# Second layer's square-ReLU inputs: two weight slots as one group, by an exact scheme of 26 block products

## The reference

```python
def sq_relu_mlp(h, w1, w2):
    return jnp.square(jax.nn.relu(h @ w1)) @ w2
# in layer l = 1
h = rmsnorm(x, norm2_g[l]) * (1.0 + sc2) + sh2
x = x + g2 * sq_relu_mlp(h, w_mlp1[l], w_mlp2[l])     # w1: 1024 x 4096, w2: 4096 x 1024
```

## Time and profile before

| | |
|---|---|
| median of 3 runs | 3288.65 us (3288.53 to 3288.9) |
| the profiled execution's own time | 3284.69 us |
| its span, first to last instruction | 3282.9 us |
| granted TensorE clock, mean | 0.999 |
| TensorE busy | 3250.7 us (99%), 15522 instructions |
| VectorE busy | 1972.2 us (60%) |
| GpSimd busy | 1031.4 us (31%) |
| ScalarE busy | 729.2 us (22%) |
| mean DMA rate | 93 GB/s |

### The profile page before, as it was taken

One profiled execution on the slowest core, in us unless ns is written; L12 is line 12 of the kernel. 1 busy time (PEld: TensorE's weight loads), 2 busy tenths in 40 slices (PEclk: granted clock), 3 DMA queues, 4 the chain that ended last, 5 costly groups with the idle time before them and its releaser, 6 DMA issues. The chain is left out here.

```text
span 3282.9 us, 40266 instructions
## 1 busy us (share of the span) xinstructions
PE 3250.7 (99%) x15522; PEld 2459.8 (75%) x15522; DVE 1972.2 (60%) x3598; ACT 729.2 (22%) x1567; POOL 1031.4 (31%) x806
## 2 busy tenths in 40 slices
PE   8999999999999999999999999999999999999999
PEld 5767775555555566788888854888886887888888
DVE  8766677676765624288545656655436588855443
ACT  3432422010101333131111124211101235321111
POOL 0111323323232010224444401444441553344443
PEclk9999999999999999999999999999999999999999
DMA  7334412333331121332222221222222221122222
GB/s 270 131 100 131 123 52 82 111 123 111 119 106 55 61 89 49 98 86 80 88 90 90 88 80 64 87 81 90 90 90 103 82 83 49 40 77 90 90 90 90
DMA packets 66895, 304.50 MB, mean 93 GB/s; under 512 B 8496, under 2 KB 21168, under 8 KB 40720
## 3 DMA queue, kind: packets, MB, share of 16 engines
q1 hardware_dynamic: 54368, 268.68, 24.1%
q0 software_dynamic: 6528, 18.75, 1.8%
q10 hardware_dynamic: 5808, 14.49, 1.3%
HBM read 292.84 MB, written 2.88 MB: 90 GB/s over the span
## 5 line engine op out<-in xcount | busy, mean ns | idle before, releaser
L2855 POOL TENSOR_TENSOR scratch<-ring 128x512 f32<-128x512 f32 (+1 forms) x160 | 226.7, 1417 | 1437.9 <-PE psum L744 957.4
L744 PE MATMUL psum<-big,scratch 128*128 128x256 f32 (+1 forms) x2240 | 606.9, 427 | 0.0
L744 PEld LDWEIGHTS psum<-big,scratch 128*128 128x128 f32 x2240 | 425.8, 190 | 163.5
L744 PE MATMUL psum<-H,scratch 128*128 128x256 f32 (+1 forms) x2144 | 498.9, 387 | 0.0
L744 PEld LDWEIGHTS psum<-H,scratch 128*128 128x128 f32 x2144 | 406.7, 190 | 76.9 <-issue 5.0
L744 PE MATMUL psum<-big,ring 128*128 128x256 f32 (+1 forms) x1584 | 421.5, 419 | 6.6 <-DVE cb L2172 2.5
L744 PE MATMUL psum<-H,ring 128*128 128x256 f32 (+1 forms) x1536 | 396.3, 400 | 1.7 <-issue 0.7
L744 PEld LDWEIGHTS psum<-big,ring 128*128 128x128 f32 x1584 | 300.3, 190 | 111.8 <-DVE cb L2172 3.7
L1480 ACT ACTIVATE cb<-psum 128x256 f32<-128x256 f32 x336 | 128.8, 383 | 1010.9 <-PE psum L744 1010.9
L744 PEld LDWEIGHTS psum<-H,ring 128*128 128x128 f32 x1536 | 290.2, 190 | 76.6 <-ACT H L1578 6.4
L713 PE MATMUL psum<-H,ring 128*128 128x512 f32 x736 | 329.6, 598 | 0.0
(11 more groups left out here) (395 smaller groups left out, 4168.5 us busy)
## 6 DMA issues: line engine op xcount, KB each, us to landing
ring<-in_wall SPq DMA_DIRECT2D x202, 1024.0 KB, 4.8
big<-in_wada SPq DMA_DIRECT2D x48, 512.0 KB, 3.5
big<-in_wada POOLq DMA_DIRECT2D x32, 512.0 KB, 4.2
big<-in_wada SPq DMA_DIRECT2D x8, 1024.0 KB, 21.1
scratch<-in_rpb ACTq DMA_DIRECT2D x16, 512.0 KB, 4.1
big<-big ACTq DMA_DIRECT2D x64, 64.0 KB, 5.1
X<-in_xin SPq DMA_DIRECT2D x4, 768.0 KB, 6.7
scratch<-negd SPq DMA_DIRECT2D x8, 384.0 KB, 9.5
```

The lines of the kernel that those rows point to most:

```text
L744: mm = pe.matmul(fast_bank(st, q, b), lhsT, rhs(k), start=start and k == 0, stop=k == kt - 1, skip_group_check=True)
L2855: pool.tensor_tensor(s1, a21, a22, ALU.add).then_inc(combo_own, 1)
```

## The change

Of the second layer's MLP the 16 "in" slots are taken as eight groups of two (`GROUPED`, `grouped_stage`); the 16 "out" slots stay as they are, and so does the first layer's MLP (`MLP[0]`).

A group is a product of a 4 x 4 grid of weight blocks (256 rows by 128 columns; rows in four parts, the 512 columns of two slots in four) with a 4 x 2 grid of input blocks (256 features by 256 tokens). It is done with 26 products of two matmuls each, and three kinds of sums:

- **inputs** (`mix_blocks`, VectorE): 18 mixed inputs of 512 columns, made inside `norm`, one after scaling 4, one after 5, one after 6, the rest after the last. They replace the 16 of 256 columns.
- **weights** (`group_weights`, GpSimd): per group 18 operations, four of 512 columns and 14 of 256, each waiting by `used(n)` until the group before has done product n with the buffer, and by `formed(n)` for its own earlier results. The ring slots of a group hold seven and six blocks of 256 columns instead of eight (1.7 MB for two). SyncE loads a further 1.3 MB of blocks (`group_terms`) and GpSimd's queue adds 0.79 MB onto them with an accumulating transfer (`accum_op`). Third form and later need its result. The ring slots are released after form 7 and form 16.
- **results**: 13 copies by ScalarE and 20 sums by VectorE per group, then eight squares and eight differences by VectorE (ScalarE's relu goes away). Products and their results use all eight banks.

TensorE's order and waits stand in `group_begins` and `group`; `group_begins` of the next group comes directly behind the group, or, behind a round's "out" slots, ahead of the last slot's last product. GpSimd's order in a round is: forms of the even group, forms of the odd group, then the four "out" slots' combinations. The rotary helper buffers move from "big" to "wx", `mixed_ready` and the counters of fast slots are renumbered, and some semaphores are shared with earlier uses.

The diff, cut to what sets the order ("..." marks what is left out):

The banks of the result chains, and TensorE's opening of a group and its product:

```diff
+chain_banks = dict(k=1, g=0, o=0, q=0, d=2, b=5, e=3, f=6, c=7, a=4)
...
+    def group_begins(st, g):
+        pe.wait_ge(group_form, W_FORMS0 + W_FORMS * g + 3)
+        if g:
...
+        times(w13, h_block(3, 1), "k")
+        if g:
+            pe.wait_ge(group_added, ADDS0 + ADDS * (g - 1) + 14)
+        times(pair_sums(g)[3], h_block(3, 0), "g")
...
+    def times(weights, inputs, to, start=True):
+        for k in range(2):
+            mm = pe.matmul(chain(to), weights[:, k * P:(k + 1) * P], inputs[:, k, :], start=start and k == 0, stop=k == 1,
+                           skip_group_check=True)
+        mm.then_inc(group_product, 1)
```

TensorE's group from product 3 on (cut):

```diff
+def group(st, g):
...
+    if g:
+        pe.wait_ge(group_added, added + 8)
+    else:
+        pe.wait_ge(h_ready, st.h0 + 4)
+    times(one21, h_block(2, 1), "d")
+    mixed(1)
+    if g:
+        pe.wait_ge(group_added, added + 13)
+    times(s03, hK, "b")
+    mixed(3)
+    if g:
+        pe.wait_ge(group_added, added + 20)
+    if after_fast:
+        pe.wait_ge(c11_done, after_fast)
+    times(w3, h3, "e")
...
+    pe.wait_ge(group_form, forms + 5)
+    pe.wait_ge(group_copied, copies + 2)
+    times(w0, hA, "g", False)
...
+    times(w14, hE, "a")
+    mixed(6)
+    pe.wait_ge(group_form, forms + 8)
+    pe.wait_ge(group_added, added + ADDS + 1)
+    times(w21, hD, "o")
...
+    mixed(16)
+    pe.wait_ge(group_added, added + ADDS + 4)
+    times(one02, h9, "q")
...
+    pe.wait_ge(group_form, forms + 18)
+    times(w7, h_block(3, 1), "e", False)
```

TensorE's order over a round:

```diff
+def grouped_stage(st):
+    group_begins(st, 0)
+    for c in range(4):
+        group(st, 2 * c)
+        group_begins(st, 2 * c + 1)
+        group(st, 2 * c + 1)
+        w.slot += 4
+        w.grouped += 4
+        fast_stage(st, None, lambda x, i: group_begins(st, 2 * c + 2) if x == 8 * c + 7 < 31 and i == 7 else None,
+                   range(8 * c + 4, 8 * c + 8))
```

What the first "out" slot of a round waits for, in TensorE's `fast_stage`:

```diff
+if st.grouped():
+    signal = {5: hid_first}.get(i, signal)
+    return lambda k, kt: pe.wait_ge(signal, st.pairs(g)) if k == 0 else None
```

VectorE's group (cut; `ready` waits for a product, a copy or a sum, `own.wait` for its own last results):

```diff
+def relu2(x, added):
+    ready(added=added)
+    own(dve.scalar_tensor_tensor(x, x, 0.0, x, ALU.max, ALU.mult))
...
+ready(product=6, copied=5)
+minus(part_m, copy_e, chain("g"))
...
+ready(product=19)
+minus(part_m, part_m, chain("d"))
+ready(product=20)
+minus(lo1[1], lo1[1], chain("f"))
+ready(added=8)
+plus(lo1[0], part_m, lo1[0])
+ready(added=9)
+minus(lo1[1], lo1[1], part_o)
+ready(copied=13)
+plus(hi1[1], copy_l, hi1[1])
+ready(product=21)
+plus(part_q, chain("b"), copy_i)
+ready(product=22, added=13)
+minus(part_m, chain("q"), part_q)
+plus(part_o, part_o, part_q)
+ready(added=14)
+plus(hi0[0], part_m, hi0[0])
+ready(added=15)
+minus(hi0[1], part_o, hi0[1])
+relu2(lo0[0], 6)
+relu2(lo0[1], 7)
+own.wait()
+dve.tensor_tensor(t0[0], lo0[1], lo0[0], ALU.subtract).then_inc(hid_first, 1)
+ready(product=24)
+plus(hi1[0], chain("c"), hi1[0])
+relu2(lo1[0], 10)
+relu2(lo1[1], 11)
+own.wait()
+dve.tensor_tensor(t1[0], lo1[1], lo1[0], ALU.subtract).then_inc(hid_first, 1)
+ready(added=18)
+plus(hi1[0], hi1[0], copy_j)
+relu2(hi0[0], 16)
+relu2(hi0[1], 17)
+own.wait()
+own(dve.tensor_tensor(t0[2], hi0[1], lo0[1], ALU.subtract))
+dve.wait_ge(hid_first, pair + 1)
+own.wait()
+dve.tensor_tensor(t0[1], hi0[1], t0[0], ALU.subtract).then_inc(hid_mid, 1)
+ready(product=26)
+minus(hi1[1], chain("e"), hi1[1])
+dve.sem_inc(hid_last, 1)
+dve.wait_ge(hid_mid, pair + 1)
+dve.tensor_tensor(t0[3], hi0[0], t0[1], ALU.subtract).then_inc(hid_mixed, 1)
```

VectorE's mixed inputs (cut), called by `norm` after each scaling:

```diff
+def mix_blocks(st, part):
...
+    if part == 4:
+        dve.wait_ge(h_ready, st.h0 + 4)
+        minus(hK, b(2, 0), b(3, 0))
+    if part == 5:
+        minus(hA, b(2, 0), b(2, 1), -1.0)
+    if part == 6:
+        formed(2)
+        plus(h3, hA, b(3, 0))
+    if part == 7:
+        formed(3)
+        minus(h5, h3, b(3, 1), -1.0)
+        dve.wait_ge(h_ready, st.h0 + 6)
+        plus(hE, b(1, 1), b(3, 1))
...
+        minus(h1, b(2, 1), hB)
```

GpSimd's forms (cut), and its order over a round:

```diff
+def group_weights(st, g):
...
+    pool.wait_ge(first_terms_in[g % 2], 16 + 48 * (g // 2 + 1))
+    row = (10240, 23040)[g % 2]
+    pool.dma_start(B_[:, row:row + 1536], wall[N_SLOTS + 2 * g + 1][:, 0:1536], accum_op=ALU.add)\
+        .then_inc(second_terms_in[g % 2], 16)
+    for i in range(2):
+        pool.wait_ge(arrived[(slot + i) % RING], 16 * ((slot + i) // RING + 1))
+    if g:
+        formed(0)
+    used(9)
+    difference(two_sums(0), two_blocks((3, 0), (0, 3)), two_blocks((1, 0), (1, 3)))
+    difference(two_sums(4), two_blocks((2, 0), (0, 2)), two_blocks((2, 1), (1, 2)))
+    pool.wait_ge(second_terms_in[g % 2], 16 * (11 + g // 2 + 1))
+    sum_of(two_sums(2), s31.unsqueeze(1).to_broadcast([P, 2, 256]), two_blocks((2, 2), (3, 3)))
+    used(15)
+    difference(w15, block(3, 1), block(3, 0))
...
+    formed(10)
+    sum_of(w4, w10, wTU)
+    used(20)
+    formed(9)
+    difference(two_sums(6), two_sums(12), block(0, 1).unsqueeze(1).to_broadcast([P, 2, 256]))
...
+    used(24)
+    formed(14)
+    sum_of(w25, wT25, w15)
+    used(26)
+    sum_of(w7, wT7, w14)
```

```diff
+for c in range(4):
+    group_weights(MLP[l], 2 * c)
+    group_weights(MLP[l], 2 * c + 1)
+    mix_weights(MLP[l], part=range(8 * c + 4, 8 * c + 8))
```

SyncE's extra loads:

```diff
+def group_terms(g):
+    if g >= 2:
+        sp.wait_ge(group_product, PRODUCTS0 + PRODUCTS * (g - 1))
+        sp.wait_ge(group_form, W_FORMS0 + W_FORMS * (g - 1))
+    at, row = (10240, 23040)[g % 2], N_SLOTS + 2 * g
+    sp.dma_start(B_[:, at:at + 1536], wall[row][:, 0:1536]).then_inc(first_terms_in[g % 2], 16)
+    at = (5120, 22016)[g % 2]
+    sp.dma_start(B_[:, at:at + 512], wall[row][:, 1536:2048]).then_inc(first_terms_in[g % 2], 16)
+    sp.dma_start(B_[:, at + 512:at + 1024], wall[row + 1][:, 1536:2048]).then_inc(first_terms_in[g % 2], 16)
```

More of the change, by code:

```diff
@@ L96, in width, with grouped, fast, fast_slots @@
         return 384 if self.wide else 256
+    def grouped(self):
+        return self.slot0 == 68
+    def fast(self, x):
+        return self.q0 + (x // 8 * 4 + x % 8 - 4 if self.grouped() else x)
+    def fast_slots(self):
+        return [x for x, (kind, g, s) in enumerate(self.slots()) if not (self.grouped() and kind == "in")]
+    def mixed0(self):
+        return 16 * self.mix + (H_FORMS - 16 if self.mix > 3 else 0)
     def slots(self):
@@ new lines, in grouped_stage, with fast_stage @@
+            def grouped_stage(st):
[8 more added lines that the diff above has]
+                               range(8 * c + 4, 8 * c + 8))
+            def fast_stage(st, y_ready=None, between=lambda x, i: None, part=None):
+                slots, s0 = st.slots(), st.slot0
+                part = part or range(len(slots))
+                assert (w.fast, w.slot) == (st.fast(part[0]), s0 + part[0])
@@ L782, in first @@
                     product(x, 1, 1, 4, lambda k: raw(0, k, 0), True, when(x, 1))
-                first(0)
-                for x in range(len(slots)):
-                    q = q0 + x
+                first(part[0])
+                for x in part:
+                    q = st.fast(x)
                     raw, mix = source(x)
@@ L820, in fast_stage @@
                     between(x, 4)
-                w.slot += len(slots)
-                w.fast += len(slots)
+                w.slot += len(part)
+                w.fast += len(part)
             def project_tokens(lhs, with_ctx, after=None, middle=None):
@@ L2102, in fast_stage, with grouped_stage @@
+            def grouped_stage(st):
+                for c in range(4):
+                    group(st, 2 * c)
+                    group(st, 2 * c + 1)
+                    w.slot += 4
+                    w.grouped += 4
+                    fast_stage(st, None, range(8 * c + 4, 8 * c + 8))
+            def fast_stage(st, between=None, part=None):
+                slots, n = st.slots(), st.width()
+                part = part or range(len(slots))
                 row, mod = st.row, mods[st.layer % 2]
@@ L2265, in to_heads @@
                     between(s, 1)
-                for x, (kind, g, s) in enumerate(slots):
+                for x in part:
+                    kind, g, s = slots[x]
+                    q = st.fast(x)
                     def modulation(x=x):
@@ L2837, in mix_weights @@
+            def mix_weights(st, after=lambda x: None, part=None):
                 nonlocal mixes
-                for x, (kind, g, s) in enumerate(st.slots()):
-                    q, slot = st.q0 + x, st.slot0 + x
+                slots = st.slots()
+                for x in part or range(len(slots)):
+                    kind, g, s = slots[x]
+                    q, slot = st.fast(x), st.slot0 + x
                     r, kt = slot % RING, st.k_half(kind, g)
@@ L3066, in _layout @@
     assert wall.shape[0] == N_SLOTS, wall.shape
+    terms = np.zeros((2 * N_GROUPS, P, SLOT), np.float32)
+    for g in range(N_GROUPS):
+        slots = [n for n, (of, i) in GROUPED.items() if of == g]
+        whole = [wall[n].reshape(P, 8, 2, P) for n in slots]
```

(7 more changed lines are left out.)

346 lines of the change are left out of this document (295 added, 51 removed).

## The result

The kernel before took 3288.78 us (median of 4 runs, 3288.53 to 3289.03), the changed one 3338.28 us (3333.9 to 3341.76): a ratio of 1.015, 95% interval 1.0132 to 1.0167. The profiled execution took 3338.05 us.

What follows compares the result with a forecast made beforehand. TensorE's count of products was taken to bound the stage. Terms -13.8 + 40 + 4.3 + 11 + 4 gave +45.5 us: 3284.7 profiled becomes 3330, and 4.0 up to the median gives 3334; range 3290 to 3348.

Steps and rivals of the forecast that it cites:

- products removed: Whole changed stage: 8 groups with 52 matmuls instead of 56 each, -13.8 us of TensorE's time.
- product 5, four times: Odd groups: product 5 waits for the even group's sum 20, late through VectorE-GpSimd contention; 10 us each, +40, bounds 0 to 46.
- turn to the output slots: First output product waits for the odd group's fourth first difference; +1.1 us, four times, +4.3.
- start, ahead of the first product: End of the stage before: GpSimd's first forms slow VectorE's two-buffer operations on the way to the normalisation, +2.3 us.
- start, up to product 10: First group: product 10 waits for sum 1 behind 18 mixed inputs, +7.1 us, and about +1.5 of contention.
- last output slots: Stage's end: VectorE's backlog beside resumed GpSimd reaches TensorE through bank waits; +4 us, 5 at most.
- an interface that VectorE keeps: Rival at product 5 of odd groups: VectorE runs undisturbed, no wait there; sum -2.4 us, 3286 us; chance 0.24.
- the price of 0.5 us for a small operation: GpSimd's 256-column form at 0.5 us: product 5 is 6 us late, +29.5, 3318 us; inside the forecast's 0.62.
- The slow transfer: Rival at product 1 of odd groups: TensorE waits if the adding transfer exceeds 9.9 us; +33.5, 3322 us; chance 0.14.

Runs made afterwards that it cites:

- e6: Changed kernel with sum 1 of the first group made behind mixed input 9 instead of behind all 18: 3328.85 us, ratio 1.0125.
- e1: Changed kernel with GpSimd's four combinations for a round's first output slot held until product 8 of the odd group: 3335.07 us, ratio 1.0141.
- e9: As e1, with both accumulating transfers of a round issued together behind the last output slot's combinations in rounds 2 to 4: 3321.84 us, ratio 1.0103.
- e2: As e1, with each of GpSimd's 18 forms per group adding 16 columns instead of 256, so most weight sums are left out: 3289.15 us, ratio 1.0006.
- e4: Changed kernel with the even group's eight squares and eight differences moved into VectorE's list for the odd group: 3310.19 us, ratio 1.0073.
- e10: Changed kernel with e6 and e7 together, two earlier ScalarE copies, e9's transfers without its held combinations, and VectorE's odd-group list reordered: 3289.11 us, ratio 1.0005.
- e11: As e10, with the second group's forms waiting until 15 of the 18 mixed inputs are made: 3283.15 us, ratio 0.999.
- e7: As e4, with e5's early transfer, and the odd group's first squares and both first differences before sums 12 to 17: 3327.72 us, ratio 1.0117.
- e5: As e1, with the odd group's accumulating transfer issued behind the even group's form 3 instead of form 18: 3344.26 us, ratio 1.0169.

## Why the prediction was right

Its forecast of +45.5 us became +49.5 between the medians and +53.4 between the profiled executions. (Its step from the profiled execution to the median, +4.0 by the runs before, fell away: the changed kernel's profiled run lies at its median.) Term by term, in us:

| term | forecast | in the profile |
|---|---|---|
| products removed | -13.8 | -13.8 |
| product 5, four times | +40 | +35.0 |
| turn to the output slots | +4.3 | +4.2 |
| start, ahead of the first product | +2.3 | +2.1 |
| start, up to product 10 | +8.7 | +9.6 |
| last output slots | +4 | +2.0 |
| clock behind the five long waits | none | +11.9 |
| earlier in the execution, behind the stage, and unassigned | | +2.3 |

The third column is from the rows above: four waits of 34.4 with 0.15 of restart each; 11.13 us against 8.99 from the last undisturbed product to the stage's first; product 10 at 1540.05 where 1528.78 was due, less the 1.7 lost before; one wait of 1.80 and a restart.

*Product 5 of the odd groups.* Right in place, engine, mechanism and nearly in size. Small GpSimd operations were 0.73 us alone and 0.90 beside VectorE (0.76 and 0.93 taken), and the operations beside them 0.83 to 0.94. In the first pair of groups GpSimd was through 31.3 us after the group's start, by the working's count (33.2 forecast), and the wait was 7.56 us. The rival of an interface that VectorE keeps fell; so did the price of 0.5 us for a small operation.

*The turn* came out as worked out, 0.89 us and the restart, with GpSimd idle.

*The start* was mis-sized in one part: the working put 1.5 us of contention over the first mixed inputs and none over the last. The last three took 1.75 us each beside the second group's forms (1534 to 1539). That sum 1 stands behind all 18 is shown by e6.

*The slow transfer* was given its own chance and another place. It took 7.0 us in the median, not the 4.5 or more of its low end nor the 9.9 from which TensorE would wait at product 1. GpSimd did wait for it, 5.4 us in each later odd group, which the forecast had named as a sign against itself. It didn't cost there; it shifted the forms into VectorE's tail. In the changed kernel most of this is hidden, since the tail is paired with the combinations anyway (8.7 to 9.4 us in the later groups against 7.6 in the first); with these out of the way it is worth 3.9 us a time (e1 against e9).

*What was missing* is the clock: nothing in the working let a wait cost more than its length. Each of the five long waits cost 2.1 to 3.0 us on top, 11.9 in all (for product 5, 5.52 to 5.79 less 3.45; for product 10, 36 instructions in 10.72 less 7.77), a quarter of the loss. The oversized +40 and +4 covered 7 of it. That the sum came closer than its parts was luck.

The Trainium skill (TensorE: Matmul & The Clock Gate, "HAM oscillation — how this bites in real kernels") warns of this, that waits between bursts of matmuls bring the slow clock back each time. By that warning the sum would have had the term; the rows agree, 0.51 to 0.64 behind every long wait.

*The lists that decide.* e2 shows that GpSimd beside VectorE makes the waits at product 5; e4, e6, e10 and e11 show that another order of the same work, with the transfers issued elsewhere in the last two, removes nearly all that TensorE waited. The saving of 13.8 us is real; it and most of the 49.5 more were lost to waits behind operations that nobody was waiting for yet, and to the clock behind them. e11's stage is 7.4 us shorter than before; 3.6 of that is lost ahead of it (12.55 us against 8.99).

## What to carry to other kernels

When a change trades TensorE's work for sums on two side engines, write each list with its due times: what releases a bank goes ahead of what is only needed a group later. Price every VectorE operation with two SBUF inputs at the length of one GpSimd operation while GpSimd is busy (0.83 to 0.94 us beside 0.90, 1.3 to 1.5 beside 1.44), and see where GpSimd's stream ends, since a transfer that it waits for moves the whole stream. And a wait of TensorE of several us costs more than its length.

## What the runs showed of the hardware

- Behind waits of 6.3 to 9.4 us the granted clock was 0.51 to 0.64 for some 5.5 us; behind 3.8 us in e1 16 instructions took 5.2 us. Behind shorter waits it went either way: 0.53 and 1.00 behind two of 1.90 us in e7, 0.68 and 1.00 behind 2.82 and 2.85 us in e5. Behind the same two waits, 1.7 and 0.92 us, it was 0.61 in the changed kernel and 1.00 in e1.
- A VectorE operation with two SBUF inputs was held for 10.8 to 11.6 us, four times in e5, when GpSimd had issued an accumulating transfer and went on with 15 operations without a wait. In e9, with idle time behind the issue, nothing was held.
- An accumulating transfer of 768 KB from GpSimd's queue landed in 7.0 us, in e9's twos in 8.5; a ring load of 896 KB in 4.7.
